# Delta rule: two scan steps of a pair ahead of the next pair's second head, three inversion steps to a place

## The chip, the cores and the metric

The kernel runs on one core of a Trainium2 chip. Its engines have queues of their own and meet only at semaphores: PE (TensorE, matmuls), ACT (ScalarE), DVE (VectorE), POOL (GpSimd) and SP (SyncE, which issues the DMAs here). The metric is the device time of one execution in microseconds (us); lower is better.

## What is computed

The program is two blocks of a model over 512 latent and 256 context tokens. The change lies in one part of the first: the gated delta rule, for 8 heads of width 128, in both directions of time, over six chunks of 128 tokens. Cut to what matters:

```python
def gdn_scan(q, k, v, g, beta, s0):
    ...
    gcum = jnp.cumsum(g, axis=-1)
    decay = jnp.exp(jnp.where(incl, gcum[..., :, None] - gcum[..., None, :], -jnp.inf))
    k_beta = k * beta[..., None]
    a_strict = jnp.where(strict, jnp.einsum('bhcik,bhcjk->bhcij', k_beta, k) * decay, 0.0)
    rhs = jnp.concatenate([v * beta[..., None], k_beta * jnp.exp(gcum)[..., None]], axis=-1)
    sol = lax.linalg.triangular_solve(a_strict, rhs, left_side=True, lower=True, unit_diagonal=True)
    u, w = sol[..., :V], sol[..., V:]
    attn = jnp.einsum('bhcik,bhcjk->bhcij', q, k) * decay
    ...
    def step(S, inp):
        qd, ke, ui, wi, ai, dec = inp
        v_new = ui - jnp.einsum('bhqk,bhkv->bhqv', wi, S)
        o = jnp.einsum('bhqk,bhkv->bhqv', qd, S) + jnp.einsum('bhqs,bhsv->bhqv', ai, v_new)
        S = S * dec[..., None, None] + jnp.einsum('bhsk,bhsv->bhkv', ke, v_new)
        return S, o
```

## The kernel before

`gdn_stage` takes the 8 heads as four pairs. Each engine runs its own list of the same named parts, unrolled in the order written; j is the pair, and a = 2j+2 and b = 2j+3 are the two heads of the next pair, which are prepared while pair j is finished. The last pair has no next one (`more` is false).

A head is prepared so: `norms` (squares, sums by a matmul with ones, L259 to L264, logarithm and exponential on ACT); `turn_v` and `turn_k` (six transposes each, L268), with `copy` on ACT (L469, L470) from banks 4 and 5 into v_tok and k_tok; `decay` on ACT (L474 for qdec, twelve exponentials in L478 for a_t); `products` on PE (L288 into bank 4, L293 into banks 6 and 7); `decayed` on DVE (attn at L628, a_t at L635, the transpose into a_turned at L641). SP then gathers the 32x32 diagonal blocks of both heads out to HBM (`gather`, L197) and loads them back as gdn_blk (`blocks_load`, L203).

The triangular matrices are inverted in levels. Level one is on DVE: `triangle(j+1, n)` for n of 0 to 30, each a product (L660) and a subtraction (L663) on the tile tri, for all blocks of the next pair at once. ACT turns the result (`turn_tri`, L489), SP scatters it out and back into y_m and x_m (`scatter`, L212 and L224), and levels five and six are matmuls on PE (L309, L322, L333, L341, L352) with copies on DVE (x_m, L670) and ACT. `weights` are 48 matmuls (L370), copied to w_neg on ACT (L518).

`steps(j)` is the scan of a pair: six steps n, two directions d, both heads. In a step PE forms v (L385, and from n = 1 on L387 with the state) into bank d, ACT scales it into v_new (L530), PE forms the addition to the state (L394) into bank 2+d, and DVE updates the state (L688 copies at n = 0, L692 later). For n of 2 and more PE also forms the output (L403, L404) into bank 6+d, which ACT copies (L539, n below 4) or DVE adds to o (L700). The triangle steps of the next pair are strewn into DVE's scan: `between()` is called twice for each n and d, ahead of the state update and behind it, and does two of them each time until all 31 are done. ACT's `turn_tri(j+1)` stands ahead of v_new of the last step. `finish` normalizes the output (L544 to L549, L707, L709).

Order within a pair: PE does weights, turn_k(b), products(b), steps, finish; ACT does weights, decay(b), copy(b, k_tok), steps, finish; DVE does decayed(a), norms(b), decayed(b), steps with the triangles, finish. SP loads the head after next once products(b) are done (kk_ready), and gathers b when a_turned_set says so.

Of the kernel before, what the change touches and what calls it, by code (L numbers as in the profile page):

```python
# [39 lines left out]
CHUNKS = TOK // P  # L40
# [68 lines left out]
def gdn_stage(nc, consts, qkvT, tabs, cum_rows, gnorm, zT, yT, blocks_in, blocks_out):  # L109
# [10 lines left out]
    with ExitStack() as ctx:  # L120
# [131 lines left out]
        def _(pe):  # L252
# [118 lines left out]
                                             start=True, stop=True)  # L371
                    last.then_inc(w_ready, 1)

            def steps(j):
                pe.wait_ge(w_set, 6 * (j + 1))
                pe.wait_ge(k_ended, 2 * (j + 1))
                pe.wait_ge(q_decayed, 2 * (j + 1))
                for n in range(CHUNKS):
                    for d in range(2):
                        c = ORDER[d][n]  # L380
                        if n > 0:
                            pe.wait_ge(s_set, S_STEPS * j + 2 * n - 1 + d)
                        for hh in range(2):
                            out = bank[d][:, hh * P:(hh + 1) * P]
                            last = pe.matmul(out, y_m[j % 2][:, hh, c, d, :], v_tok[(2 * j + hh) % 4][:, c, :], start=True, stop=(n == 0))  # L385
                            if n > 0:
                                last = pe.matmul(out, w_neg[:, hh, c, d, :], state[:, (n - 1) % 2, hh, d, :], start=False, stop=True)  # L387
                        last.then_inc(v_ready, 1)
                    for d in range(2):
                        c = ORDER[d][n]  # L390
                        pe.wait_ge(v_set, STEPS * j + 2 * n + d + 1)
                        if n < CHUNKS - 1:
                            for hh in range(2):
                                last = pe.matmul(bank[2 + d][:, hh * P:(hh + 1) * P], k_end[:, hh, c, d, :], v_new[:, hh, d, :],  # L394
                                                 start=True, stop=True)
                            last.then_inc(s_ready, 1)
                        if c >= CTX_CHUNKS:
                            at = 2 * (n - CTX_CHUNKS) + d
                            if at >= 2:
                                pe.wait_ge(o_set, O_STEPS * j + at - 1)  # L400
                            for hh in range(2):
                                out = bank[6 + d][:, hh * P:(hh + 1) * P]
                                pe.matmul(out, state[:, (n - 1) % 2, hh, d, :], qdec[(2 * j + hh) % 4][:, c - 2, d, :], start=True, stop=False)  # L403
                                last = pe.matmul(out, v_new[:, hh, d, :], attn[(2 * j + hh) % 4][:, c - 2, d, :], start=False, stop=True)  # L404
                            last.then_inc(o_ready, 1)
# [11 lines left out]
            for j in range(PAIRS):  # L417
                more = j + 1 < PAIRS
                a, b = 2 * j + 2, 2 * j + 3
                if more:  # L420
                    norms(a)
                level5_t(j)
                if more:
                    turn_v(a)
                level5_x(j)
                level5_y(j)
                if more:
                    turn_k(a)
                level6_t(j, 0)
                level6_t(j, 1)  # L430
                if more:
                    products(a)
                level6_y(j, 0)
                level6_y(j, 1)
                if more:
                    norms(b)
                    turn_v(b)
                weights(j, 0)
                weights(j, 1)
                if more:  # L440
                    turn_k(b)
                    products(b)
                steps(j)
                finish(j)

        @block.scalar
        def _(act):
# [70 lines left out]
                    act.activation(w_neg[:, hh, 2 * b:2 * b + 2].rearrange("p c d q -> p (c d q)"), bank[(3, 0, 1, 2)[n % 4]][:, :],  # L518
                                   ACT.Copy, scale=-1.0).then_inc(w_set, 1)

            def steps(j):
                for n in range(CHUNKS):
                    if n == CHUNKS - 1 and j + 1 < PAIRS:
                        turn_tri(j + 1)
                    for d in range(2):
                        c = ORDER[d][n]
                        act.wait_ge(v_ready, STEPS * j + 2 * n + d + 1)
                        for hh in range(2):
                            hd = 2 * j + hh
                            ins = act.activation(v_new[:, hh, d, :], bank[d][:, hh * P:(hh + 1) * P], ACT.Copy,  # L530
                                                 scale=tabs[:, 0, c, d, hd:hd + 1])
                        ins.then_inc(v_set, 1)
                    for d in range(2):
                        c = ORDER[d][n]
                        if 2 <= n < 4:
                            act.wait_ge(o_ready, O_STEPS * j + 2 * (n - 2) + d + 1)
                            if n == 2 and d == 0 and j > 0:
                                act.wait_ge(stored, 32 * j)
                            act.activation(o[:, :, (c - 2) * P:(c - 1) * P], bank[6 + d][:, 0:256].rearrange("p (h q) -> p h q", h=2),  # L539
                                           ACT.Copy).then_inc(o_set, 1)  # L540
# [13 lines left out]
            for j in range(PAIRS):  # L554
                more = j + 1 < PAIRS
                a, b = 2 * j + 2, 2 * j + 3
                if more:
                    norms(a)
                level5_t(j)
                if more:  # L560
                    copy(a, v_tok[a % 4], v_turned, v_copied)
                    decay(a)
                level5_y(j)
                if more:
                    copy(a, k_tok[a % 4], k_turned, k_copied)
                level6_t(j, 0)
                level6_t(j, 1)
                level6_y(j, 0)
                level6_y(j, 1)
                if more:  # L570
                    norms(b)
                    copy(b, v_tok[b % 4], v_turned, v_copied)
                weights(j)
                if more:
                    decay(b)
                    copy(b, k_tok[b % 4], k_turned, k_copied)
                steps(j)
                finish(j)

        @block.gpsimd  # L580
# [28 lines left out]
        def _(dve):  # L609
# [60 lines left out]
                        dve.tensor_scalar(x_m[g2, :, :, d, g1].rearrange("p h c q -> p (h c) q"),  # L670
                                          bank[2][g2, 0:384].rearrange("p (x q) -> p x q", q=B32), -1.0, None, ALU.mult).then_inc(x5_set, 1)

            def steps(j, between):
                for n in range(CHUNKS):
                    for d in range(2):
                        c = ORDER[d][n]
                        between()
                        if n < CHUNKS - 1:
                            dve.wait_ge(s_ready, S_STEPS * j + 2 * n + d + 1)
                            if n >= 2:  # L680
                                dve.wait_ge(s_set, S_STEPS * j + 2 * n + d - 1)
                                if n >= 4:
                                    dve.wait_ge(o_ready, O_STEPS * j + 2 * (n - 4) + d + 1)
                            for hh in range(2):
                                hd = 2 * j + hh
                                s_new = bank[2 + d][:, hh * P:(hh + 1) * P]
                                if n == 0:
                                    ins = dve.tensor_copy(state[:, 0, hh, d, :], s_new)  # L688
                                else:
                                    if n == 1:  # L690
                                        dve.wait_ge(s_set, S_STEPS * j + d + 1)
                                    ins = dve.scalar_tensor_tensor(state[:, n % 2, hh, d, :], state[:, (n - 1) % 2, hh, d, :],  # L692
                                                                   tabs[:, 3, c, d, hd:hd + 1], s_new, ALU.mult, ALU.add)
                            ins.then_inc(s_set, 1)
                        between()
                        if n >= 4:
                            dve.wait_ge(o_ready, O_STEPS * j + 2 * (n - 2) + d + 1)
                            dve.wait_ge(o_set, O_STEPS * j + 4)
                            cols = slice((c - 2) * P, (c - 1) * P)
                            dve.tensor_tensor(o[:, :, cols], o[:, :, cols], bank[6 + d][:, 0:256].rearrange("p (h q) -> p h q", h=2),  # L700
                                              ALU.add).then_inc(o_set, 1)
# [15 lines left out]
            for j in range(PAIRS):  # L717
# [10 lines left out]
                if more:  # L728
                    decayed(a)
                    norms(b)  # L730
                    decayed(b)
                at = [0]

                def between():

                    for _ in range(2 if more else 0):
                        if at[0] < TRI_STEPS:
                            triangle(j + 1, at[0])
                            at[0] += 1

                steps(j, between)
                finish(j)


# [2490 lines left out]
```

## Time and profile before

| what | value |
|---|---|
| time of three runs | median 4553.44 us (4553.36 to 4560.42) |
| the profiled execution, its own time | 4547.87 us |
| its span, first to last instruction | 4546.1 us |
| mean granted TensorE clock | 0.91 of full speed |
| PE busy in the span | 3797.5 us, 84% |
| PE weight loads | 3079.6 us, 68% |
| DVE busy | 1872.7 us, 41% |
| ACT busy | 1507.0 us, 33% |
| the delta rule's pairs, L309 of the first to L309 of the fourth | 1243.87 to 1559.67 us from the start |

The shares are means over stages with different limits; the delta rule is some 400 us of the span. A timeline row gives start and length in us, the engine, the line of the kernel, the operation with output and inputs, how many instructions were merged into the row, and in brackets how long the engine was idle before it and what ended that.

### The profile page before, as it was taken

To read this page: it belongs to the slowest core of one execution; us is meant where nothing else is said; L and a number is where in the kernel's file an instruction comes from. 1 tells how busy PE (TensorE), PEld (TensorE's weight loads), DVE (VectorE), ACT (ScalarE), POOL (GpSimd) and SP (SyncE) were. 2 spreads that over 40 slices of the span, in tenths; PEclk is the share of its full clock that TensorE was granted. 3 is DMA by queue.
4 is the path that set the end of the run, shared out by engine and by line. 5 is a ranking of instruction groups with operands and counts; after the bars stand their busy time and mean duration, and the time that the engine had idled before them with its cause. 6 is when DMAs were issued, how large, how long until landed. Compare 5 with 4: busy or idle time off the path is not lost. (4 is left out here: it accounts for less than half of the span.)

```text
span 4546.1 us, 53169 instructions
## 1 busy us (share of the span) xinstructions
PE 3797.5 (84%) x20530; PEld 3079.6 (68%) x20530; DVE 1872.7 (41%) x2775; ACT 1507.0 (33%) x2348; POOL 347.9 (8%) x257
## 2 busy tenths in 40 slices
PE   6939999997255665958999988878899999979696
PEld 2128888885254554847888867766689887868485
DVE  1043444431445444245455553243553344432344
ACT  0042222221244333225565552242422343431331
POOL 0020000000111034021010110001000000000000
PEclk9958999998578787979999999989999999989798
DMA  7702322242222102324222215132554454542131
GB/s 280 262 24 83 93 84 90 81 127 59 72 63 81 29 34 85 125 71 134 82 90 81 86 54 188 56 98 66 99 117 118 107 99 99 102 123 97 47 106 56
DMA packets 477416, 437.24 MB, mean 96 GB/s; under 512 B 56347, under 2 KB 415004, under 8 KB 475948
## 3 DMA queue, kind: packets, MB, share of 16 engines
q1 hardware_dynamic: 461472, 389.57, 30.7%
q10 hardware_dynamic: 11292, 27.81, 1.6%
q0 software_dynamic: 4464, 17.30, 1.1%
q8 instruction: 124, 2.03, 0.2%
q14 instruction: 64, 0.52, 0.0%
HBM read 379.22 MB, written 55.36 MB: 96 GB/s over the span
## 5 line engine op out<-in xcount | busy, mean ns | idle before, releaser
L1576 PE MATMUL o_acc<-y_in_hi,o_w_hi 128*128 128x512 f32 x768 | 301.9, 393 | 65.5 <-DVE o_w_lo L1698 65.5
L2154 DVE TENSOR_TENSOR od_w_lo<-od_w,od_w_hi 128x512 fp32r<-128x512 f32 x260 | 178.9, 698 | 402.9 <-ACT od_w_hi L2147 402.1
L2131 PE MATMUL od_acc<-od_u_hi,od_w_hi 128*128 128x512 f32 x784 | 318.5, 406 | 24.0 <-DVE od_u_lo L2260 19.1
L1576 PE MATMUL p_acc<-u_hi,p_w_hi 128*128 128x512 f32 x832 | 327.8, 394 | 2.8 <-DVE p_w_lo L1698 2.8
L1583 PE MATMUL p_acc<-u_hi,p_w_lo 128*128 128x512 f32 x832 | 328.1, 394 | 0.0
L1577 PE MATMUL p_acc<-u_lo,p_w_hi 128*128 128x512 f32 x832 | 324.4, 390 | 0.0
L2132 PE MATMUL od_acc<-od_u_lo,od_w_hi 128*128 128x512 f32 x784 | 312.1, 398 | 0.0
L2133 PE MATMUL od_acc<-od_u_hi,od_w_lo 128*128 128x512 f32 x784 | 311.7, 398 | 0.0
L1577 PE MATMUL o_acc<-y_in_lo,o_w_hi 128*128 128x512 f32 x768 | 301.2, 392 | 0.0
L1583 PE MATMUL o_acc<-y_in_hi,o_w_lo 128*128 128x512 f32 x768 | 301.1, 392 | 0.0
L2131 PE MATMUL ev_acc<-ev_u_hi,ev_w_hi 128*128 128x512 f32 x640 | 266.7, 417 | 39.0 <-DVE ev_u_lo L2260 38.1
L2147 ACT ACTIVATE od_w_hi<-od_w 128x512 fp32r<-128x512 f32 x260 | 161.1, 628 | 416.5 <-PE od_acc L2133 252.3
L1743 DVE TENSOR_TENSOR p_w_lo<-p_w,p_w_hi 128x1024 fp32r<-128x1024 f32 x100 | 121.9, 1225 | 392.8 <-ACT p_w_hi L1638 392.6
L2132 PE MATMUL ev_acc<-ev_u_lo,ev_w_hi 128*128 128x512 f32 x640 | 254.6, 398 | 0.0
L2133 PE MATMUL ev_acc<-ev_u_hi,ev_w_lo 128*128 128x512 f32 x640 | 254.4, 398 | 0.0
L1743 DVE TENSOR_TENSOR o_w_lo<-o_w,o_w_hi 128x1024 fp32r<-128x1024 f32 x84 | 102.8, 1226 | 309.6 <-ACT o_w_hi L1638 309.6
L1638 ACT ACTIVATE p_w_hi<-p_w 128x1024 fp32r<-128x1024 f32 x100 | 105.5, 1060 | 355.7 <-PE p_acc L1583 342.7
L2154 DVE TENSOR_TENSOR ev_w_lo<-ev_w,ev_w_hi 128x512 fp32r<-128x512 f32 x192 | 136.7, 739 | 204.9 <-ACT ev_w_hi L2147 204.5
L1576 PE MATMUL g_acc<-h_hi,g_w_hi 128*128 128x512 f32 x512 | 201.2, 393 | 18.7 <-DVE g_w_lo L1698 18.7
L1576 PEld LDWEIGHTS o_acc<-y_in_hi,o_w_hi 128*128 128x128 f32 x768 | 145.9, 190 | 97.9 <-DVE o_w_lo L1698 67.6
L1577 PE MATMUL g_acc<-h_lo,g_w_hi 128*128 128x512 f32 x512 | 200.9, 392 | 0.0
L1583 PE MATMUL g_acc<-h_hi,g_w_lo 128*128 128x512 f32 x512 | 200.8, 392 | 0.0
(543 smaller groups left out, 8457.9 us busy)
## 6 DMA issues: line engine op xcount, KB each, us to landing
od_w<-in_o_w_in_dram SPq DMA_DIRECT2D x260, 256.0 KB, 5.1
p_w<-in_w_in_dram SPq DMA_DIRECT2D x104, 512.0 KB, 3.8
mod_w<-in_w_ada_dram SPq DMA_DIRECT2D x12, 4096.0 KB, 13.6
ev_w<-in_e_w_in_dram SPq DMA_DIRECT2D x192, 256.0 KB, 2.9
g_w<-in_ple_gate_w_dram SPq DMA_DIRECT2D x64, 512.0 KB, 3.4
o_w<-in_w_out_dram SPq DMA_DIRECT2D x32, 512.0 KB, 3.6
o_w<-in_e_w_out_dram SPq DMA_DIRECT2D x32, 512.0 KB, 3.6
o_w<-in_o_w_out_dram SPq DMA_DIRECT2D x32, 512.0 KB, 3.4
```

The lines of the kernel that those rows point to most:

```text
L1576: pe.matmul(lat, wh, x_hi[:, k, lat0:tokens], start=first, stop=False)
L1577: pe.matmul(lat, wh, x_lo[:, k, lat0:tokens], start=False, stop=False)
L1583: last = pe.matmul(lat, wl, x_hi[:, k, lat0:tokens], start=False, stop=end)
L1638: act.activation(w_hi[r][:], w[r][:], ACT.Copy).then_inc(hi_s, 1)
L1743: dve.tensor_tensor(w_lo[r][:], w[r][:], w_hi[r][:].bitcast(F32), ALU.subtract).then_inc(lo_s, 1)
L2131: pe.matmul(out, hi, self.x_hi[:, k, :], start=first, stop=False)
L2132: pe.matmul(out, hi, self.x_lo[:, k, :], start=False, stop=False)
L2133: last = pe.matmul(out, lo, self.x_hi[:, k, :], start=False, stop=end)
L2147: act.activation(self.w_hi[m % self.ring][:], self.w[m % self.ring][:], ACT.Copy).then_inc(self.hi_set, 1)
L2154: eng.tensor_tensor(self.w_lo[m % self.ring][:], self.w[m % self.ring][:], self.w_hi[m % self.ring][:].bitcast(F32), ALU.subtract).then_in ...
```

## The change

PE, ACT and DVE do steps 0 and 1 of the scan of pair j ahead of what they still have to do for head b: PE ahead of turn_k(b) and products(b), ACT behind decay(b) and ahead of copy(b, k_tok), DVE ahead of decayed(b). Steps 2 to 5 follow. PE waits for a_set of head b ahead of step 2, since the products of b are read from banks 6 and 7, which the output of the scan uses from step 2 on. The triangle steps begin with step 2, and three instead of two go into each place. `decayed` of head a, and everything in SP's and POOL's lists, stay in place.

```diff
@@ PE
-            def steps(j):
-                pe.wait_ge(w_set, 6 * (j + 1))
-                pe.wait_ge(k_ended, 2 * (j + 1))
-                pe.wait_ge(q_decayed, 2 * (j + 1))
-                for n in range(CHUNKS):
+            def steps(j, lo, hi):
+                if lo == 0:
+                    pe.wait_ge(w_set, 6 * (j + 1))
+                    pe.wait_ge(k_ended, 2 * (j + 1))
+                    pe.wait_ge(q_decayed, 2 * (j + 1))
+                elif j + 1 < PAIRS:
+                    pe.wait_ge(a_set, 4 * (j + 2))
+                for n in range(lo, hi):
...
                 weights(j, 0)
                 weights(j, 1)
+                steps(j, 0, 2)
                 if more:
                     turn_k(b)
                     products(b)
-                steps(j)
+                steps(j, 2, CHUNKS)
                 finish(j)
@@ ACT
                 if more:
                     decay(b)
+                steps(j, 0, 2)
+                if more:
                     copy(b, k_tok[b % 4], k_turned, k_copied)
-                steps(j)
+                steps(j, 2, CHUNKS)
                 finish(j)
@@ DVE
                 if more:
                     decayed(a)
                     norms(b)
-                    decayed(b)
                 at = [0]
 
                 def between():
 
-                    for _ in range(2 if more else 0):
+                    for _ in range(3 if more else 0):
                         if at[0] < TRI_STEPS:
                             triangle(j + 1, at[0])
                             at[0] += 1
 
-                steps(j, between)
+                steps(j, 0, 2, lambda: None)
+                if more:
+                    decayed(b)
+                steps(j, 2, CHUNKS, between)
                 finish(j)
```

## Rows read from the trace of the kernel before

**Rows 1.** the page: the span and the first line of busy time

```profile
span 4546.1 us, 53169 instructions
```

**Rows 2.** busy time by stretch, L309 of one pair to the next's

```profile
core 0: us, PE busy (x) PEld busy (x) DVE busy (x) ACT busy (x) POOL busy (x), PEclk, DMA share, GB/s
...
1243.87:1349.33 105.46, 60.89 (x704) 52.31 (x704) 46.56 (x126) 43.74 (x98) 12.58 (x6) 0.82 0.22 60
1349.33:1454.90 105.57, 62.00 (x704) 53.07 (x704) 52.45 (x131) 44.05 (x99) 12.58 (x6) 0.79 0.24 66
1454.90:1559.67 104.77, 60.51 (x699) 53.43 (x699) 53.22 (x131) 40.27 (x92) 9.18 (x5) 0.77 0.20 53
```

**Rows 3.** one line of the waits in 1243 to 1560: us, times, longest

```profile
DVE gdn_part L660 <- DMA gdn_blk<-s_blocks_in: 25.3, 3, 8.6
```

**Rows 4.** timeline, first pair, around head b: start, length, engine, line

```profile
1288.24 0.58 ACT L469 ACTIVATE gdn_k_tok<-gdn_bank 128x512 f32<-128x512 f32 x1
...
1289.14 2.08 PE L288 MATMUL gdn_bank<-gdn_q_n,gdn_k_n 128*128 128x128 f32 x8 [5.22 <-ACT gdn_k_tok L470]
...
1291.33 1.23 DVE L628 TENSOR_TENSOR gdn_attn<-gdn_bank,gdn_a_t 128x1024 f32<-128x1024 f32 x1 [13.39 <-PE gdn_bank L288]
1292.83 3.19 DVE L635 SCALAR_TENSOR_TENSOR gdn_a_t<-gdn_bank,gdn_tabs,gdn_a_t 128x128 f32<-128x128 f32 x12 [0.28 <-PE gdn_bank L293]
...
1305.66 0.20 DVE L660 TENSOR_TENSOR gdn_part<-gdn_blk,gdn_tri 96x31 f32<-96x31 f32 x1 [8.62 <-DMA gdn_blk<-s_blocks_in]
```

**Rows 5.** timeline of the first inversion, which has no scan beside it

```profile
1203.17 0.20 DVE L660 TENSOR_TENSOR gdn_part<-gdn_blk,gdn_tri 96x31 f32<-96x31 f32 x1 [10.44 <-DMA gdn_blk<-s_blocks_in]
...
1226.04 0.19 DVE L663 TENSOR_TENSOR gdn_tri<-gdn_tri,gdn_part 96x31 f32<-96x31 f32 x1
...
1226.26 1.98 ACT L489 ACTIVATE gdn_blk<-gdn_tri 96x1024 f32<-96x1024 f32 x1 [41.68 <-DVE gdn_tri L663]
```

**Rows 6.** timeline of the end of the second inversion and of L309 behind it

```profile
1331.55 0.19 DVE L663 TENSOR_TENSOR gdn_tri<-gdn_tri,gdn_part 96x31 f32<-96x31 f32 x1
...
1332.66 0.63 ACT L530 ACTIVATE gdn_v_new<-gdn_bank,gdn_tabs 128x128 f32<-128x128 f32 x2 [0.33 <-PE gdn_bank L387]
...
1333.18 2.01 ACT L489 ACTIVATE gdn_blk<-gdn_tri 96x1024 f32<-96x1024 f32 x1
...
1349.34 1.02 PE L309 MATMUL gdn_bank<-gdn_x_m,gdn_a_t 32*32 32x32 f32 x96 [1.75 <-DMA gdn_y_m<-s_blocks_out]
```

**Rows 7.** timeline of the scan in the fourth pair, without triangles

```profile
1581.07 1.14 ACT L530 ACTIVATE gdn_v_new<-gdn_bank,gdn_tabs 128x128 f32<-128x128 f32 x4 [0.80 <-PE gdn_bank L385]
...
1583.04 0.49 PE L385 MATMUL gdn_bank<-gdn_v_tok,gdn_y_m 128*128 128x128 f32 x2
...
1584.24 0.63 ACT L530 ACTIVATE gdn_v_new<-gdn_bank,gdn_tabs 128x128 f32<-128x128 f32 x2 [2.02 <-PE gdn_bank L387]
...
1586.33 0.30 PEld L385 LDWEIGHTS gdn_bank<-gdn_v_tok,gdn_y_m 128*128 128x128 f32 x2
```

**Rows 8.** timeline: six transposes, scan products, products of another head

```profile
1277.06 0.84 PE L268 MATMUL gdn_bank<-k_ident,gdn_raw_v 128*128 128x128 f32 x6 [2.17 <-issue]
...
1277.94 0.60 ACT L469 ACTIVATE gdn_v_tok<-gdn_bank 128x512 f32<-128x512 f32 x1 [0.98 <-PE gdn_bank L268]
...
1309.86 0.80 PE L385 MATMUL gdn_bank<-gdn_v_tok,gdn_y_m 128*128 128x128 f32 x2 [0.73 <-DVE gdn_state L688]
...
1311.98 0.62 ACT L530 ACTIVATE gdn_v_new<-gdn_bank,gdn_tabs 128x128 f32<-128x128 f32 x2 [2.18 <-PE gdn_bank L387]
...
1362.45 1.91 PE L288 MATMUL gdn_bank<-gdn_q_n,gdn_k_n 128*128 128x128 f32 x8
```

**Rows 9.** busy time by stretch: products of b, first step 1 beside triangles

```profile
1289.00:1293.20 4.20, 4.06 (x22) 4.06 (x23) 1.59 (x3) 0.09 (x1) 0.00 (x0) 0.60 0.01 4
...
1305.60:1309.00 3.40, 1.95 (x8) 1.78 (x8) 3.04 (x13) 0.00 (x0) 0.00 (x0) 0.50 0.00 0
```

**Rows 10.** timeline of the x_m copies of the second pair

```profile
1355.46 2.31 DVE L670 TENSOR_SCALAR gdn_x_m<-gdn_bank 32x384 f32<-32x384 f32 x4
```

More of the change, by code:

```diff
@@ L519, in weights, with steps @@
                                    ACT.Copy, scale=-1.0).then_inc(w_set, 1)
-            def steps(j):
-                for n in range(CHUNKS):
+            def steps(j, lo, hi):
+                for n in range(lo, hi):
                     if n == CHUNKS - 1 and j + 1 < PAIRS:
@@ L671, in level5_x, with steps @@
                                           bank[2][g2, 0:384].rearrange("p (x q) -> p x q", q=B32), -1.0, None, ALU.mult).then_inc(x5_set, 1)
-            def steps(j, between):
-                for n in range(CHUNKS):
+            def steps(j, lo, hi, between):
+                for n in range(lo, hi):
                     for d in range(2):
```

## The prediction, made before the change was run

> **What bounds the kernel now.** The change touches one stage, the delta rule (gdn_stage), so I read in this order: the page for the span [rows 1], the busy time by stretch from one pair's inversion products (L309) to the next pair's [rows 2], the waits in these three stretches [rows 3], and then the timeline around the moved code [rows 4 to 8], the granted clock there [rows 9] and one place behind it [rows 10].
>
> The stage has a regular period: 105.46, 105.57 and 104.77 us from L309 of one pair to L309 of the next [rows 2]. In each, PE is busy 60 to 62 us and DVE 47 to 53 us: no engine is full, so the period is a chain of waits and I have to find it. It closes like this, for the first pair (times in us from the span's start). ACT ends the decay of the second head b of the next pair and copies k_tok from 1288.24. PE's products of b wait for that copy (idle 5.22) and start at 1289.14. DVE waits for them, 13.39, starts attn at 1291.33, scales a_t from 1292.83 for 3.19 and transposes [rows 4]. The blocks go out to HBM and come back, DVE waits 8.62 for gdn_blk, and the 31 triangle steps begin at 1305.66 [rows 4]; over the three pairs this wait is 25.3 us, at most 8.6 [rows 3]. The last triangle step ends at 1331.55+0.19 = 1331.74, ACT turns the triangle from 1333.18, the result is scattered and read back, and PE waits for that DMA before L309 at 1349.34 [rows 6]. L309 leads, in program order on PE and ACT, to the weights of this pair and so to the decay and copy of b again. So what lies between the decay of b and the triangles is paid in full, once for each of the three pairs that have a next one. The fourth pair has none and its order does not change.
>
> **The change part by part.** It has three pieces: steps 0 and 1 of the scan go in front of turn_k and products of b (PE), of copy(b, k_tok) (ACT) and of decayed(b) (DVE); three triangle steps instead of two go into each place; PE waits for a_set of b before step 2.
>
> Steps 0 and 1, moved forward: in the old order they cost nothing on the way to the triangles, since they come behind the products. In the new one they stand in front. PE can do the first products of step 0 while ACT is still in the decay, but v_new(0) on ACT is queued behind it, so the steps begin where the copy began, at 1288.24. Their length without triangles is to be seen in the fourth pair: v_new(0) from 1581.07, first weight load of step 2 at 1586.33, so PE is free after 5.26 us [rows 7]. Then come the six transposes of turn_k; they were hidden under the decay and are so no more: 1277.06 to the copy at 1277.94 is 0.88 for the same six with v [rows 8]. Together +6.14 us before the copy, the products, the attn and a_t of DVE, the gather of SP, the load of gdn_blk, and every triangle step. Behind them in SP's queue stands the load of the head after next, which waits for the products of b too; POOL has nothing before its next need.
>
> The clock: PE is idle 5.22 us and then runs the products mostly at the lower of its two clocks, 1.2 in place of 2.4 GHz: the granted clock of that stretch is 0.60, and 0.50 in step 1 behind the long wait [rows 9]. Eight products took 2.08 [rows 4] where the same eight took 1.91 for another head [rows 8]; DVE waits another 0.28 for L293 [rows 4]. In the new order PE has an idle of some 4 us ahead of k_end of step 0, and the slow spell can fall on steps 0 and 1. What that costs: eight instructions L385/L387 up to v_new took 1311.98-1309.86 = 2.12 slow [rows 8] and 1584.24-1583.04 = 1.20 fast [rows 7], so 0.92 for eight, 0.115 each. Some 30 instructions of PE stand on the new way (4 L394, 16 L385/L387, 4 L394, 6 L268), so all slow is +3.45; none slow is 0, and as the products would then be fast, -0.17-0.28 = -0.45. I take one group of eight slow and the products fast: 0.92-0.45 = +0.47, nearest to the spell seen. The page TensorE: Matmul & The Clock Gate of the Trainium skill (section Part 1, The HAM clock gate) says that the array falls to half rate after idling and comes back after being busy. By that rule the slow spell follows the idle, and the trace agrees [rows 4, 9]. If the rule is taken to say that the matmuls filled into the idle keep the clock, the term is -0.45 in place of +0.47 and the whole sum 2.8 us lower.
>
> Triangles, three to a place: a step costs the same, and DVE is not waiting during them, so only what is strewn between counts. Back to back, the 31 steps of the first inversion took 1203.17 to 1226.04+0.19, 23.06 us [rows 5]. In the scan they took 1331.74-1305.66 = 26.08, so the eight state updates among them cost 3.02, 0.38 each. In the new order eleven places do; they begin at step 2, hold five state updates and one addition into o, at 0.38 each 2.28. Gain 0.74. Does the scan keep up with three? A triangle step is 23.06/31 = 0.74 on the mean. Between two updates of one direction lie twelve of them, some 9 us, and between update (3,1) and update (4,0), which PE's order ties together, six, 4.5 us; a scan step alone takes 3.3 us (L385 from 1583.04 to 1586.33 [rows 7]). It keeps up.
>
> The turn: now ACT finishes v_new of step 4 before the turn and PE had to wait for the last state update for it, so the turn starts 1333.18-1331.74 = 1.44 after the last triangle step [rows 6]; after the first inversion, with ACT free, 0.03 [rows 5]. In the new order v_new(4) needs state update (3,1), which is nine triangle steps before the last, so it is done. Gain 1.41.
>
> The wait for a_set on PE: it falls away under the DMA round trip of 8.6 us that follows; behind it stand the products of step 2, and ACT's v_new and DVE's state update behind those, some 3 us of work, within that cover. Cost nothing; without the cover up to 3 us. The load of gdn_blk, and the scatter with its round trip, I leave as they are. The tail after the turn starts with more of the scan done, up to 1.4 us ahead, and has slack already, as PE waits 1.75 for DMA at L309 [rows 6]. DVE comes to the x_m copies of the next pair without an idle of its own [rows 10], so it may have ended last there, and a tail that is ahead could give back up to 1.4 per pair, at least 0; I take 0, as PE's L322 feeds them as well.
>
> Sum for one pair: +6.14 +0.47 -0.74 -1.41 = +4.46; three pairs +13.4 us. The profiled execution's own time is 4547.87, 1.8 more than its span of 4546.1 [rows 1], and would be 4561.3; the median of the three runs shown is 5.6 above it, so I forecast 4553.4+13.4 = 4566.8. About 0.2%, 9.1 us or 3.0 per pair, is what a measurement of this kernel can tell from no change.
>
> **The rivals.** A, no measurable change: the clock stays full (-0.45 in place of +0.47), the wait for gdn_blk is 0.5 shorter each time, as in one of the three pairs now (25.3 less twice 8.6 is 8.1 [rows 3]), and the x_m copies give 0.5 of their 1.4. Then 2.5 per pair, +7.6, 4561. For it: each term is seen somewhere in the trace [rows 3, 9, 10]. Against it: it needs all of them on one side.
>
> B, faster: the round trip of the blocks is not released by the products of b, but by something that the change does not delay. Then the 6.14 falls away and the 2.15 stay, with the clock's 0.45 and the 0.5 of the read-back 3.1 per pair: -9.3, 4544. It decides from the point where that other release is 6 us later than the products. Against it: DVE goes from attn to the transpose without a pause longer than 0.28 and waits for L288 itself, and SP gathers only what DVE has turned [rows 4].
>
> C, slower than forecast: steps 0 and 1 run at half clock throughout (+3.45 in place of +0.47), 7.4 per pair, +22.3, 4575.7. For it: PE is idle again and again in this stretch, and steps with gaps ran slow [rows 8, 9].
>
> D, the change does not do what it says: three to a place let the scan fall behind, DVE waits for PE between triangles, and the 0.74 and 1.41 are lost: 6.6 per pair, +19.8, 4573. The stretch between updates, worked out above, speaks against it.
>
> **How the numbers follow.** Forecast as worked out, +9 to +18: 0.58. C and D, which share their side: 0.17. A: 0.18. B: 0.07. Slower by over 0.2% is the forecast with C and D, 0.75; within 0.2% A, 0.18; faster B, 0.07. The range leaves out B, the lower third of A and the far end of C: 4556 to 4577.
>
> **What would show it.** In the changed kernel the copy of k_tok for b starts some 6 to 8 us after the end of the decay, right behind v_new of step 1; the wait of DVE for gdn_blk is still 8 to 9 us; from the first to the last triangle step 25.3 us; the turn follows within 0.1; the period is near 109.7. If the copy starts less than 5 us after the decay, or DVE no longer waits for gdn_blk, the chain as told is wrong. If DVE is idle between triangle steps, D holds. If the period has grown and L309 no longer waits for a DMA, the tail has become the bound, which I have costed at nothing.

## The result, and the profile after

The changed kernel takes 4567.54 us, median of 20 runs (4558.46 to 4577.22), against 4555.3 for 20 runs of the kernel before beside it (4548.56 to 4564.5). The ratio is 1.0027, with a 95% interval of 1.0020 to 1.0034: it is slower, by 12.2 us on the medians. Forecast were +13.4 us and 4566.8.

The page of the profiled execution after, the span and the busy times:

```profile
span 4575.2 us, 53172 instructions
...
PE 3817.1 (83%) x20530; PEld 3096.8 (68%) x20530; DVE 1873.4 (41%) x2775; ACT 1506.8 (33%) x2348; POOL 346.7 (8%) x257
```

Nothing was added to the work: matmuls, DVE and ACT have the counts and, but for PE's slow spells, the busy times of before. The span is longer all the same, so what grew is waiting. Busy time by stretch, from L309 of one pair to L309 of the next, the same three stretches as [rows 2] (the columns are those of [rows 2]):

```profile
1244.20:1355.74 111.54, 68.82 (x704) 58.91 (x705) 48.00 (x127) 43.21 (x98) 12.60 (x6) 0.77 0.21 57
1355.74:1471.17 115.43, 68.10 (x705) 58.21 (x705) 53.25 (x131) 44.77 (x100) 12.59 (x6) 0.76 0.22 63
1471.17:1581.45 110.28, 63.41 (x698) 56.22 (x698) 52.34 (x131) 39.44 (x91) 9.18 (x5) 0.76 0.19 48
```

The periods are 111.54, 115.43 and 110.28 us in place of 105.46, 105.57 and 104.77. That is more than the forecast 109.7, and more than the medians allow: this execution is 9 us over its own median and the one before was 7 us under its own. Which stretches swing like this from one execution to the next is told with the table further down.

The timeline of the changed kernel around head b in the first pair (start, length, engine, line; the decay is L478 and L482, L534 is v_new, L397 the addition to the state, L473 the copy of k_tok, L634 attn), which answers to [rows 4]:

```profile
1286.04 1.05 ACT L478 ACTIVATE gdn_qdec<-gdn_crow 128x1024 f32<-128x1024 f32 x1
...
1286.99 3.60 ACT L482 ACTIVATE gdn_a_t<-gdn_a_t,gdn_ncum 128x128 f32<-128x128 f32 x12
...
1290.49 1.11 ACT L534 ACTIVATE gdn_v_new<-gdn_bank,gdn_tabs 128x128 f32<-128x128 f32 x4
...
1291.14 2.08 PE L397 MATMUL gdn_bank<-gdn_v_new,gdn_k_end 128*128 128x128 f32 x8 [3.79 <-ACT gdn_v_new L534]
...
1297.65 0.82 PE L268 MATMUL gdn_bank<-k_ident,gdn_k_n 128*128 128x128 f32 x6
...
1298.51 0.60 ACT L473 ACTIVATE gdn_k_tok<-gdn_bank 128x512 f32<-128x512 f32 x1 [1.46 <-PE gdn_bank L268]
...
1299.43 1.16 PE L288 MATMUL gdn_bank<-gdn_q_n,gdn_k_n 128*128 128x128 f32 x8 [0.96 <-ACT gdn_k_tok L474]
...
1300.69 1.22 DVE L634 TENSOR_TENSOR gdn_attn<-gdn_bank,gdn_a_t 128x1024 f32<-128x1024 f32 x1 [2.24 <-PE gdn_bank L288]
1301.95 3.19 DVE L641 SCALAR_TENSOR_TENSOR gdn_a_t<-gdn_bank,gdn_tabs,gdn_a_t 128x128 f32<-128x128 f32 x12
...
1305.20 0.49 PE L388 MATMUL gdn_bank<-gdn_v_tok,gdn_y_m 128*128 128x128 f32 x2 [3.27 <-DVE gdn_a_t L641]
...
1314.29 0.20 DVE L666 TENSOR_TENSOR gdn_part<-gdn_blk,gdn_tri 96x31 f32<-96x31 f32 x1 [8.13 <-DMA gdn_blk<-s_blocks_in]
```

The start of the decay in the kernel before, in the same pair:

```profile
1283.79 1.05 ACT L474 ACTIVATE gdn_qdec<-gdn_crow 128x1024 f32<-128x1024 f32 x1
```

The reader is to see the queue. v_new of step 0 starts the moment the decay is through, at 1290.49; PE has been idle 3.79 for it. The transposes L268 come behind the last L397 of step 1, the copy at 1298.51. From the start of the decay's first instruction, 1286.04, that is 12.47 us, where before it was 4.45 (the copy at 1288.24 [rows 4]). Everything behind follows in the same order: products, attn, a_t, the wait for gdn_blk, here 8.13. The products are faster than before (1.16 for 2.08), and a_t comes 1.26 behind attn, before it was 1.50. PE's new wait for a_set is the 3.27 ahead of L388 at 1305.20, nine us ahead of the first triangle step, and so under the DMA's way.

The granted clock of TensorE in the two halves of that stretch (the clock stands ahead of the last two numbers):

```profile
1291.00:1295.60 4.60, 4.46 (x20) 4.43 (x21) 0.98 (x4) 1.14 (x5) 0.00 (x0) 0.50 0.01 4
1295.60:1299.40 3.80, 2.60 (x20) 2.17 (x18) 1.21 (x4) 1.58 (x5) 0.00 (x0) 0.96 0.00 0
```

It is 0.50, the lower of the two levels (1.2 GHz), from 1291.0 to 1295.6, behind the idle of 3.79, and 0.96 on the mean of the next 3.8 us.

The end of the triangles and the tail, which answer to [rows 6]:

```profile
1339.36 0.19 DVE L669 TENSOR_TENSOR gdn_tri<-gdn_tri,gdn_part 96x31 f32<-96x31 f32 x1
...
1339.58 1.98 ACT L493 ACTIVATE gdn_blk<-gdn_tri 96x1024 f32<-96x1024 f32 x1 [5.21 <-DVE gdn_tri L669]
...
1344.55 1.06 ACT L548 ACTIVATE gdn_o_sq<-gdn_o 128x1024 f32<-128x1024 f32 x1 [2.08 <-DVE gdn_o L706]
...
1355.74 1.02 PE L309 MATMUL gdn_bank<-gdn_x_m,gdn_a_t 32*32 32x32 f32 x96 [1.40 <-DMA gdn_y_m<-s_blocks_out]
```

The same instruction of the tail (the square of the output) in the kernel before:

```profile
1339.48 1.06 ACT L544 ACTIVATE gdn_o_sq<-gdn_o 128x1024 f32<-128x1024 f32 x1 [1.70 <-DVE gdn_o L700]
```

The turn, L493, follows 0.03 after the last triangle step has ended at 1339.55, no longer 1.44. The scan's tail reaches the square of the output 4.97 after the start of the turn; in the kernel before it was 6.30. PE still waits for the DMA ahead of L309, so nothing comes of that.

### The profile page after: what moved, and what is told of

Its sections match the earlier page's. It is cut to its first block and busy times, and to the rows that moved or that the text cites. A ratio compares the mean times of both kernels' runs of the same rounds, so it can differ in the third digit from the quotient of the medians.

```text
span 4575.2 us, 53172 instructions
## 1 busy us (share of the span) xinstructions
PE 3817.1 (83%) x20530; PEld 3096.8 (68%) x20530; DVE 1873.4 (41%) x2775; ACT 1506.8 (33%) x2348; POOL 346.7 (8%) x257
```

## The experiments

All compare with the kernel before, run beside them on the same chip. To read them together I cut the three periods of each profile at the same places: L309, the start of the decay of b, the copy of k_tok of b, attn of b, the first triangle step, the last one, the turn, the next L309. Sums of the three pairs in us, from one profile of each run:

```
                 to decay  to copy  to attn  to first  to last   to    to    sum
                                             triangle  triangle turn  L309
before             118.9    13.3      9.3     42.6      77.7     4.9  49.2  315.8
changed            125.4    37.2      6.6     42.0      75.2     0.7  50.3  337.2
after_again        124.9    36.6      6.6     43.5      75.2     0.7  50.4  337.8
after_third        117.0    36.4      6.6     43.3      75.2     0.7  50.9  330.1
in_wait            122.5    13.3      9.2     45.0      75.3     0.7  50.5  316.5
in_wait_again      121.2    13.3      9.3     45.4      75.3     0.7  50.5  315.6
one_step           122.1    25.5      7.5     43.4      79.2     0.7  50.4  328.8
copy_first         122.8    -2.3     16.0     40.8      77.7     4.9  49.7  309.6
both               124.5    -2.3     16.0     42.3      75.3     0.7  50.1  306.6
three_only         123.0    13.3      9.2     45.4      73.9    20.8  49.5  335.2
warm               119.2    31.7      6.6     43.3      75.2     0.7  49.8  326.5
warm_again         122.6    31.7      6.6     43.2      75.2     0.7  50.4  330.4
fill_seven         120.3    31.7      6.6     42.7      75.2     0.7  49.4  326.7
```

Four columns hardly move within a kernel: to the copy (within 0.8 over three pairs), to attn, to the last triangle, to the turn. They hold the change. The first, fourth and last swing from one execution to the next: the same changed kernel has 125.4, 124.9 and 117.0 up to the decay. The kernel before has one kept profile, and its 118.9 is at the low end: the six profiles that start as it does (in_wait twice, copy_first, both, three_only and itself) have 122.2 on the mean, the seven with a step moved forward 121.6. So the change itself does nothing visible to that column.

One source of the swing is the 48 products of the weights, L370. Their row in the first pair, with the stretch that they fill and its granted clock, from the changed kernel and then from after_third, the same kernel:

```profile
1277.93 7.58 PE L370 MATMUL gdn_bank<-gdn_y_m,gdn_w_neg 128*128 128x128 f32 x48
...
1277.93:1285.51 7.58, 7.58 (x49) 7.39 (x48) 0.00 (x0) 3.86 (x7) 0.00 (x0) 0.72 0.00 0
```

```profile
1275.61 5.52 PE L370 MATMUL gdn_bank<-gdn_y_m,gdn_w_neg 128*128 128x128 f32 x48
...
1275.61:1281.13 5.52, 5.52 (x50) 5.33 (x48) 0.20 (x1) 3.86 (x7) 0.00 (x0) 1.00 0.00 0
```

PE is busy without a pause in both; what differs is the clock, 0.72 on the mean against 1.00. In every pair of the thirteen profiles the two go together: where these 48 take 5.52 the clock is 1.00, where they take 7.15 it is 0.76. Both come in one and the same kernel. What decides it is not shown.

So a difference of some us in one profile's period says little, and the time is judged on medians, the mechanism on the four steady columns.

### after_again, after_third: the changed kernel again

> The changed kernel once more, beside the others. Chain theory (what stands between the decay and the copy of k_tok of head b is paid in full by each of three pairs): 12 to 15 us over before, from the start of the decay of b to the copy of k_tok 12.4 us in each pair, not 4.45. Rival, code placement (the loss comes from pauses of PE in its instruction stream ahead of and in the weights, which in the one profile were 2.2 us a pair longer from L309 to the decay of b): the stretch from L309 to the decay of b is again 41.8, 43.0, 40.6 us, not 39.9, 40.3, 38.7; by the chain theory it falls to either set by chance.

> The changed kernel beside its variant with the filled idle, on one chip. 12 to 14 us over before. Copy of k_tok of b 11.9 to 12.5 behind the start of its decay.

The ratios are 1.0030 (1.0018 to 1.0043; 4570.87 against 4556.36) and 1.0026 (1.0016 to 1.0036; 4563.94 against 4555.57). The copy comes 12.46, 12.28 and 11.85, then 11.85, 12.30 and 12.21 behind the start of the decay. The stretch up to the decay was as long as in the first profile once and shorter than before's the other time (117.0 against 118.9), so the rival, that the loss comes from where the weights' code lies, falls: the code is the same in all three, and the stretch is not. The copy came about half a us sooner in two of the six pairs than the 12.4 expected of each; step 0's L397 took 1.84 there in the first pair of after_third, and 2.08 in the first pair of the changed kernel.

### one_step: a smaller dose

```diff
-                steps(j, 0, 2)
+                steps(j, 0, 1)
...
-                steps(j, 2, CHUNKS)
+                steps(j, 1, CHUNKS)
```

(on PE, ACT and DVE alike, and two triangle steps to a place again)

> As the change, but only step 0 stands ahead of head b, and two triangles go into each place of steps 1 to 4. Chain theory: v_new(0) and the products of L397 take 2.7 and the six transposes 0.9, so +3.6 to the copy in place of +8.0; products at full clock -0.9, triangles +0.4, turn -1.4: +1.7 per pair, 5 us over before. Rival, a fixed price for any split (the new wait of PE for a_set, transposes no longer hidden, code placement): nearly the whole 12 us stays.

The timeline of the first pair:

```profile
1286.92 3.60 ACT L482 ACTIVATE gdn_a_t<-gdn_a_t,gdn_ncum 128x128 f32<-128x128 f32 x12
...
1291.08 2.07 PE L397 MATMUL gdn_bank<-gdn_v_new,gdn_k_end 128*128 128x128 f32 x8 [3.79 <-ACT gdn_v_new L534]
...
1294.47 0.60 ACT L473 ACTIVATE gdn_k_tok<-gdn_bank 128x512 f32<-128x512 f32 x1 [2.94 <-PE gdn_bank L268]
...
1296.66 1.22 DVE L634 TENSOR_TENSOR gdn_attn<-gdn_bank,gdn_a_t 128x1024 f32<-128x1024 f32 x1 [2.98 <-PE gdn_bank L288]
```

The ratio is 1.0016 (1.0007 to 1.0025; 4565.86 against 4556.36), +7 by the ratio, where 5 were expected. The copy comes 8.50 behind the start of the decay, +4.05 and not +3.6, as L397 ran slow, in 2.07; the steady columns give (25.5-13.3) + (7.5-9.3) + (79.2-77.7) + (0.7-4.9) = +7.7 for three pairs, against +14.5 for the whole change: (37.2-13.3) + (6.6-9.3) + (75.2-77.7) + (0.7-4.9). One step costs about half of two. A fixed price for the split of nearly the whole 12 us is excluded; a small one is not.

### in_wait: the same two steps, but in DVE's wait

```diff
-                steps(j, between)
+                steps(j, 0, 2, lambda: None)
+                steps(j, 2, CHUNKS, between)
```

(DVE alone, behind decayed(b), with three to a place; PE and ACT as before)

> PE and ACT keep the order of before; only DVE differs: decayed(b), then steps 0 and 1 without triangles, then steps 2 to 5 with three to a place. So the two steps run in DVE's wait for gdn_blk, not ahead of the products. Chain theory: the copy of k_tok stays 4.45 behind the start of the decay, the triangles take 25.0 in place of 25.9 and the turn follows at once (1.41 saved): 2.2 to 2.3 less per pair, 6.7 us under before and some 20 under the change. Rival, the loss comes from the scan being split and three triangles in a place: 12 us over before as with the change.

> The two steps in the wait for gdn_blk, again, since the first comparison's interval reached from 0.9982 to 1.0000. Chain theory: triangles and turn save 2.2 per pair, 6.7 us under before, 0.9985.

DVE in the first pair, from the transpose to the first triangle step:

```profile
1298.83 0.98 DVE L641 STREAM_TRANSPOSE gdn_sq_k<-gdn_a_t 128x768 f32<-128x768 f32 x1
1299.73 0.84 DVE L688 COPY gdn_state<-gdn_bank 128x128 f32<-128x128 f32 x4
...
1303.76 0.61 DVE L692 SCALAR_TENSOR_TENSOR gdn_state<-gdn_state,gdn_tabs,gdn_bank 128x128 f32<-128x128 f32 x2 [0.29 <-PE gdn_bank L394]
...
1309.29 0.20 DVE L660 TENSOR_TENSOR gdn_part<-gdn_blk,gdn_tri 96x31 f32<-96x31 f32 x1 [4.93 <-DMA gdn_blk<-s_blocks_in]
```

Here the steps cost nothing: from L688 at 1299.73 to the last L692 at 1303.76 they lie where DVE used to wait 8.62 [rows 4], and 4.93 of that wait is left. The three steady gains of the change are kept (triangles 75.3, turn 0.7) and the copy is where it was. The times are 4551.88 against 4556.36 (ratio 0.9991, 0.9982 to 1.0000) and 4551.33 against 4554.69 (0.9996, 0.9987 to 1.0005). The loss of the change is gone for certain, which the rival (the split or three to a place is to blame) excludes. The gain of 6.7 over before is not shown by itself: -4.1 and -1.8 by the ratios, and the second interval just misses 0.9985. In the two profiles the way from attn to the first triangle is 2.4 and 2.8 longer over three pairs and the last column 1.3. Three_only, which up to the first triangle runs the order of the kernel before, has 45.4 there as well, so that much can come by chance; whether it did in in_wait is open.

### copy_first: what the chain gives if it is shortened

```diff
                 if more:
-                    decay(b)
                     copy(b, k_tok[b % 4], k_turned, k_copied)
+                    decay(b)
```

(on ACT, in the kernel before)

> The kernel before with one edit: ACT copies k_tok of b ahead of the decay of b and not behind it; no scan step moves. Chain theory: the products of b run under the decay, attn starts when the decay ends, 5.3 after the last weights copy and not 7.5, and a_t without its 0.28: 2.5 less per pair, 7.4 us under before. Rival (the products of b are released by something else, the blocks' way is not on the chain): no change.

ACT, PE and DVE in the first pair:

```profile
1286.02 0.60 ACT L469 ACTIVATE gdn_k_tok<-gdn_bank 128x512 f32<-128x512 f32 x1
...
1286.94 1.16 PE L288 MATMUL gdn_bank<-gdn_q_n,gdn_k_n 128*128 128x128 f32 x8 [0.96 <-ACT gdn_k_tok L470]
1287.72 3.60 ACT L478 ACTIVATE gdn_a_t<-gdn_a_t,gdn_ncum 128x128 f32<-128x128 f32 x12
...
1291.36 1.22 DVE L628 TENSOR_TENSOR gdn_attn<-gdn_bank,gdn_a_t 128x1024 f32<-128x1024 f32 x1 [12.99 <-ACT gdn_a_t L478]
...
1292.62 3.19 DVE L635 SCALAR_TENSOR_TENSOR gdn_a_t<-gdn_bank,gdn_tabs,gdn_a_t 128x128 f32<-128x128 f32 x12
```

The products of b run at 1286.94 under the decay, and attn starts with the end of the decay, no longer with PE: 5.34 behind the copy's start in place of 7.54 behind the decay's [rows 4], and a_t without its 0.28. The ratio is 0.9978 (0.9969 to 0.9987; 4545.13 against 4556.36), -10 by the ratio; the 7.4 expected lie within the interval. This is the same chain pulled the other way, so the rival, that the products of b do not release the blocks, is out.

### three_only: three to a place without the move

```diff
-                    for _ in range(2 if more else 0):
+                    for _ in range(3 if more else 0):
```

> The kernel before with three triangle steps to a place in place of two, nothing else. Chain theory: the triangles take 24.9 in place of 25.9, but ACT turns them behind v_new of step 4, and with the triangles in steps 0 to 2 two scan steps stand between: the turn starts 5 to 6 behind the last triangle, 3 more per pair in all, 9 us over before. Rival, three to a place is a gain by itself: 3 us under before.

ACT and DVE at the end of the triangles in the first pair:

```profile
1334.34 0.19 DVE L663 TENSOR_TENSOR gdn_tri<-gdn_tri,gdn_part 96x31 f32<-96x31 f32 x1
...
1340.76 0.62 ACT L530 ACTIVATE gdn_v_new<-gdn_bank,gdn_tabs 128x128 f32<-128x128 f32 x2 [0.27 <-PE gdn_bank L387]
...
1341.28 2.01 ACT L489 ACTIVATE gdn_blk<-gdn_tri 96x1024 f32<-96x1024 f32 x1
```

The last triangle step has ended at 1334.53, but the turn stands behind v_new of step 4 and starts at 1341.28, 6.75 later, and 6.94 behind the last step's start where it was 1.63. The ratio is 1.0027 (1.0016 to 1.0037; 4568.68 against 4557.38). Triangles -3.8 and turn +15.9 make +12.1 for three pairs, where +9 was expected. Three to a place needs the scan to be two steps ahead; by itself it is a loss.

### warm, warm_again, fill_seven: PE's idle filled

```diff
+                    for _ in range(fill if n == 0 else 0):
+                        pe.matmul(bank[6][:, 0:256], ident[:], neg[:].rearrange("p d q -> p (d q)"), start=True, stop=True)
```

(in PE's steps, behind the first products of step 0; fill is 8, or 7 in fill_seven; each of them stands in the profile as two matmuls)

> The changed kernel, and PE fills its idle ahead of L397 of step 0 with eight matmuls of 256 columns of constants into bank 6, whose result nobody reads. If the part of the delay beyond the counted 6.14 is the low clock, the stretch from the start of the decay to the copy of k_tok falls from 12.3 to 12.5 down to 10.6, 1.7 less per pair, 5 us under the change. Rival: the extra 1.9 is the semaphores' way between engines that the fourth pair's rows did not show; then it stays at 12.4.

> The change with PE's idle filled, again. In its first run the stretch from the decay to the copy fell from 12.4 to 10.57 in all three pairs, but the time did not fall with it. If the 1.8 per pair is on the chain, this run is 5 us under the changed kernel of the same call, the first comparison having lain across two calls. Rival: the filling costs elsewhere what it gives here, and the two are equal within 2 us.

> The change with seven filling matmuls in place of eight. In both runs with eight, the delta rule was 5 to 10 us shorter than the changed kernel's, but from the last output of the delta rule to the end of the program it took 2952.7 and 2955.6 in place of 2943.8 to 2948.6, most of it in waits of the odd block, whose code is not touched. If that comes from where the added instructions push the later code, one less moves it again: the rest falls back to some 2946 and the run is 5 us under the changed kernel, 1.0016 of before. If it comes from the filling as such (power, clock, a bank), the rest stays at 2953 or more.

The first pair of warm (L393 are the filling matmuls, L399 the addition to the state), and its busy time with the granted clock:

```profile
1281.71 3.62 PE L393 MATMUL gdn_bank<-k_neg,k_ident 128*128 128x256 f32 x16
...
1285.01 1.11 ACT L536 ACTIVATE gdn_v_new<-gdn_bank,gdn_tabs 128x128 f32<-128x128 f32 x4
...
1285.67 1.22 PE L399 MATMUL gdn_bank<-gdn_v_new,gdn_k_end 128*128 128x128 f32 x8 [0.34 <-ACT gdn_v_new L536]
...
1290.28 0.82 PE L268 MATMUL gdn_bank<-k_ident,gdn_k_n 128*128 128x128 f32 x6
...
1291.13 0.60 ACT L475 ACTIVATE gdn_k_tok<-gdn_bank 128x512 f32<-128x512 f32 x1 [1.46 <-PE gdn_bank L268]
```

```profile
1286.00:1290.00 4.00, 3.74 (x30) 3.35 (x29) 1.39 (x6) 1.37 (x5) 0.00 (x0) 1.00 0.00 0
```

The clock is 1.00, and the copy comes 10.57 behind the start of the decay in all nine pairs of the three profiles, within 0.01: 4.45 + 6.12, the counted 6.14. So of the 7.4 to 8.0 by which the move delays the copy, 6.1 is the work itself and the rest, 1.3 to 1.9, is the clock at 0.50. But the time does not follow: 1.0036 (1.0024 to 1.0048), 1.0035 (1.0021 to 1.0048) and 1.0040 (1.0026 to 1.0054), where 1.0016 was expected. Warm_again took 4572.95 where the changed kernel beside it, after_third, took 4563.94. The profiles show that the delta rule did get shorter, 326.5, 330.4 and 326.7 in place of 337.2, 337.8 and 330.1 (of which the steady columns give 5 and the rest is swing), and that it is lost later, as told in the last section.

### both: the two gains together

This is in_wait and copy_first in one kernel.

> The kernel before with both edits that gained: the two scan steps in DVE's wait for gdn_blk with three triangles to a place after them, and the copy of k_tok of b ahead of its decay. The two act on different pieces of the chain, so the chain theory adds them: 2.2 and 2.7 per pair, 14 to 15 us under before. Rival: once the triangles come earlier, the tail of the scan and the next pair's sums are the bound at L309, and the idle of PE there no longer ends with a DMA; then 8 to 10 us.

ACT and DVE of the first pair:

```profile
1283.01 0.60 ACT L469 ACTIVATE gdn_k_tok<-gdn_bank 128x512 f32<-128x512 f32 x1
...
1288.35 1.22 DVE L628 TENSOR_TENSOR gdn_attn<-gdn_bank,gdn_a_t 128x1024 f32<-128x1024 f32 x1 [14.15 <-ACT gdn_a_t L478]
...
1299.91 0.61 DVE L692 SCALAR_TENSOR_TENSOR gdn_state<-gdn_state,gdn_tabs,gdn_bank 128x128 f32<-128x128 f32 x2 [0.38 <-PE gdn_bank L394]
...
1301.69 0.20 DVE L660 TENSOR_TENSOR gdn_part<-gdn_blk,gdn_tri 96x31 f32<-96x31 f32 x1 [1.18 <-DMA gdn_blk<-s_blocks_in]
```

It takes 4539.71 us against 4557.38 (ratio 0.9964, 0.9950 to 0.9978), -16.4 by the ratio, and beats both kernels. The two scan steps now fill the wait for gdn_blk almost wholly in this pair: 1.18 of it is left, 3.21 and 1.95 in the others. PE still waits for the DMA at the three L309 that follow, 13.0 in all, so the rival, a tail that takes over, did not come.

## Why the prediction was right

**The chain.** The claim that everything between the decay of b and the triangles is paid in full, three times, held. The dose (one_step), the removal (in_wait) and the reversal (copy_first) all move the time the way it says. The exception is the gain of the filled kernels, which the stage shows and the whole does not.

**Steps 0 and 1 in front: +6.14 for the work.** With the clock held up it is 6.12 in nine pairs of nine.

**The clock: +0.47, right in sum only because two errors cancel.** The term was one group of eight at the low clock, +0.92, less 0.45 for products that turn fast. The first half was too small: over the nine pairs of the three profiles of the changed kernel the copy comes 7.8 later on the mean, 1.65 beyond the 6.14, since the low clock lay on all of step 0's L397 (2.08 for eight in the first pair) and most of step 1. The second half was too small as well. The 1.91 that I took for the fast price of the eight products was itself a slow one: the granted clock from 1362.40 to 1364.40 was 0.58, and at full clock they take 1.16. So attn came 2.19 behind the copy and not 3.09, a gain of 0.90 for the 0.17, and a_t followed attn after 1.26 where it had been 1.50, 1.47 and 1.71, a gain of 0.3 for the 0.28. Together 1.65-0.90-0.30 = 0.45. That this meets 0.47 is luck.

PE came back slow from an idle of 3.79 and was fast where warm left it none. The Trainium skill says that the array drops to half rate after idling (TensorE: Matmul & The Clock Gate, Part 1: The HAM clock gate). The traces agree: 0.50 behind the idle, 1.00 in warm. The reading that the moved matmuls would keep the clock themselves was wrong, since they left that idle in front of them.

**Triangles: -0.74.** Measured -0.83 (25.07 for 25.89), and from the first step to the end of the last 25.26, forecast 25.3. The scan kept up: no profile of the changed kernel shows DVE idle between the first and the last triangle step. D did not come.

**The turn: -1.41.** Measured 1.41.

**The wait for a_set, the tail: nothing.** Both held; PE's wait at L309 still ended with the DMA, and in_wait, which lacks the wait for a_set, has the same 75.3 and 0.7 behind it.

**The sum.** The steady columns make +14.5, +13.9 and +13.7 over three pairs in the three profiles. The quicker a_t, which they leave out, takes 0.9 off, so the mean is +13.1. The forecast was 13.4, the medians say 12.2. What failed was the use of one profile for the period: I said 109.7, and the profiles of the changed kernel have 110.0 to 112.6 on the mean. The steady columns account for +4.8 a pair at most; the rest lies in the columns that swing, above all the one up to the decay, where the profile of before was low.

**The rivals.** A asked for the clock to stay full; it did not. B asked for another release of the blocks; copy_first excludes it. C, the low clock throughout, came half true: 1.65 of its 3.45, before the gains behind it.

## What to carry to other kernels

Work that fills an idle engine is free only if it stands behind the instruction that starts the longest wait of the chain; put in front of that instruction it is paid in full, though the engines look as idle there. The same two scan steps delayed the chain by 7.4 to 8.0 us a pair ahead of the products and by nothing that the steady columns show in the wait that follows them. When several engines share a chain, look at each queue for an instruction that others wait for and that stands behind one that nobody needs yet (the copy behind the decay): that swap alone gave 10 us, more than the two scan steps gave in their best place.

## What the runs showed of the hardware that was not expected

PE waits in the program's other block (tiles od_), some 1600 us behind the delta rule, in code that no edit touches, and these waits grew in the filled kernels. Waits of PE there, from 3180 to 4075, in after_third and then in warm (us in all, times, longest):

```profile
PE od_bank L2926 <- DMA od_v_tok<-s_v: 14.1, 3, 6.9
PE od_bank L2907 <- DVE od_tabs L3049: 6.9, 1, 6.9
```

```profile
PE od_bank L2928 <- DMA od_v_tok<-s_v: 20.3, 4, 9.0
PE od_bank L2909 <- DVE od_tabs L3051: 10.2, 1, 10.2
```

All three filled kernels have it: 9.7 to 10.4 for od_tabs in place of 6.9, 9.0 in place of 6.1 for the last od_v_tok (6.9 is the longest of the three in after_third). From the last pair's square of o to the end of the span it takes 2955.6, 2952.7 and 2957.1 us; the ten other profiles here have 2941.7 to 2948.6. The means are 2955.1 and 2945.1: 10 us, more than the 5 that the clock gave back. The kernels differ from the changed one only in the 42 or 48 matmuls of the profile added in the delta rule. One matmul less to a pair did not bring it back, which speaks against a mere shift of the code by so much, but it is a weak test; the cause is open.

The other is the swing itself: the same instructions, L370 x48, took 5.52 or 7.58 us at one place as the granted clock over them was 1.00 or 0.72, and the stretch from L309 to the decay took 117.0 to 125.4 us over three pairs of one kernel. A single profile of this kernel can't tell 5 us.
